# Summing two and a half of six modulation weights on GpSimd instead of VectorE

## The reference, cut to what matters

```python
mod_x = (jax.nn.silu(c) @ w_mod[i] + b_mod[i])[:, None, :]     # 1024 -> 6144
sh1x, sc1x, g1x, sh2x, sc2x, g2x = jnp.split(mod_x, 6, axis=-1)
hx = modulate(rmsnorm(x, norm1_g[i]), sh1x, sc1x)
...
x = x + g1x * out_x
hx2 = modulate(rmsnorm(x, norm2_g[i]), sh2x, sc2x)
x = x + g2x * peer(hx2, ...)
```

## Time and profile before

| | us |
|---|---|
| median of 3 runs | 1464.42 |
| profiled execution, whole | 1466.92 |
| its span | 1464.9 |
| TensorE busy | 1320.8 |
| VectorE busy | 1109.2 |
| ScalarE busy | 636.5 |
| GpSimd busy | 311.1 |

### The profile page before, as it was taken

One profiled execution on the slowest core, in us unless ns is written; L12 is line 12 of the kernel. 1 busy time (PEld: TensorE's weight loads), 2 busy tenths in 40 slices (PEclk: granted clock), 3 DMA queues, 4 the chain that ended last, 5 costly groups with the idle time before them and its releaser, 6 DMA issues.

```text
span 1464.9 us, 16512 instructions
## 1 busy us (share of the span) xinstructions
PE 1320.8 (90%) x5504; PEld 879.2 (60%) x5504; DVE 1109.2 (76%) x2316; ACT 636.5 (43%) x1322; POOL 311.1 (21%) x308
## 2 busy tenths in 40 slices
PE   9998899897897979697987799999999999999998
PEld 3876655453342534253443346678888877788887
DVE  6688857966767776776667677869997577799974
ACT  5344733322222222222222126567776445777752
POOL 0000004344444333344434330001110000011100
PEclk9999999999898989898898899999999999999999
DMA  9624468999999999999999996434445434355540
GB/s 394 268 115 195 158 246 346 415 421 422 419 421 421 422 421 421 420 412 421 418 421 400 417 386 262 172 116 171 174 174 200 160 118 157 115 182 200 193 144 29
DMA packets 50436, 416.31 MB, mean 284 GB/s; under 512 B 5552, under 2 KB 5680, under 8 KB 7088
## 3 DMA queue, kind: packets, MB, share of 16 engines
q0 software_dynamic: 36864, 268.45, 44.3%
q1 hardware_dynamic: 13488, 146.82, 26.2%
HBM read 414.20 MB, written 1.05 MB: 283 GB/s over the span
## 4 chain that ended last, share of the span: by engine, by line
PE 54%; DVE 21%; DMA 15%; issue 5%; ACT 3%; POOL 2%; DVEq 0%; SPq 0%; POOLq 0%; ACTq 0%
PE ps L1510 11%; PE ps L1223 9%; DMA ring<-in_uv,ids 8%; PE ps L1512 6%; DMA arena<-in_uv,ids 5%; PE ps L1302 4%; PE ps L1304 4%; PE ps L1303 4%; DVE ring L2260 4%; DVE arena L2260 2%; DMA ring<-in_b1w 2%; PE ps L1045 2%; PE ps L934 2%; PE ps L936 2%; PE ps L935 2%
## 5 line engine op out<-in xcount | busy, mean ns | idle before, releaser
L1223 PE MATMUL ps<-ring,arena 128*128 128x512 f32 x632 | 297.3, 621 | 53.1 <-ACT arena L1736 53.1
L2260 DVE CUSTOM_DVE_ANT_0 ring<-ring,arena 128x1024 f32<-128x1024 f32 x158 | 190.5, 1223 | 84.9 <-DMA ring<-in_uv,ids 84.2
L1223 PEld LDWEIGHTS ps<-ring,arena 128*128 128x128 f32 x632 | 123.7, 199 | 216.3 <-issue 152.4
L1510 PE MATMUL ps<-hpair,arena_r 128*128 128x512 f32 x704 | 249.0, 399 | 0.0
L617 DVE TENSOR_TENSOR arena_r<-ring,arena_r 128x1024 fp32r<-128x1024 f32 x152 | 185.6, 1224 | 61.3 <-ACT arena_r L602 58.5
L1223 PE MATMUL ps<-arena 128*128 128x512 f32 x392 | 189.2, 628 | 47.3 <-ACT arena L1736 47.1
L819 POOL DMA_INDIRECT ring<-in_uv,ids x158 | 168.5, 1066 | 233.7 <-PE ps L1223 176.3
L1512 PE MATMUL ps<-hpair,arena_r 128*128 128x256 f32 x704 | 198.0, 281 | 0.0
L602 ACT ACTIVATE arena_r<-ring 128x1024 fp32r<-128x1024 f32 x152 | 159.2, 1054 | 60.0 <-PE ps L1304 57.9
L819 POOL DMA_INDIRECT arena<-in_uv,ids x98 | 104.4, 1065 | 353.6 <-issue 240.2
L1223 PEld LDWEIGHTS ps<-arena 128*128 128x128 f32 x392 | 77.9, 202 | 150.2 <-issue 92.9
(11 more groups left out here) (337 smaller groups left out, 2037.5 us busy)
## 6 DMA issues: line engine op xcount, KB each, us to landing
ring<-in_lw SPq DMA_DIRECT2D x39, 2048.0 KB, 7.8
ring<-in_b1w SPq DMA_DIRECT2D x14, 2048.0 KB, 8.7
ring<-in_b1w SPq DMA_DIRECT2D x9, 1024.0 KB, 16.9
ring<-in_lw SPq DMA_DIRECT2D x8, 1024.0 KB, 5.1
wqb<-in_wq SPq DMA_DIRECT2D x4, 1024.0 KB, 9.0
arena<-in_wq SPq DMA_DIRECT2D x3, 1024.0 KB, 13.4
ring<-in_uv,ids POOLq DMA_INDIRECT x158, 16.8
ring<-in_lw SPq DMA_DIRECT2D x2, 1088.0 KB, 10.0
```

The lines of the kernel that those rows point to most:

```text
L1223: last = nc.tensor.matmul(ps[:, 4 + 2 * c + b, :], diag[:, k % 4, :], vrows[place(n, k)][:, b * 512:(b + 1) * 512], start=(n == c and k == 0),
L1510: nc.tensor.matmul(ps[:, bank, :].rearrange("p (t n) -> p t n", t=2), high_of(l, p)[:, cols_], hpair[:, :, k, :], start=(k == 0), stop=Fal ...
L2260: V.tensor_tensor_reduce(out=urows[at], in0=urows[at], in1=hrow[:, c, :], scale=1.0, scalar=0.0, op0=ALU.mult, op1=ALU.add, accum_out=dots ...
```

## The change

Weights 1 and 3 and the second half (k = 4 to 7) of weight 5 are summed by GpSimd in accumulator 1; weights 0, 2, 4 and the first half of weight 5 by VectorE in accumulator 0. GpSimd's sum uses two instructions for a part, a product into a new buffer `mterm` (the number of the partition is spread over 512 columns by a broadcast) and an addition to the accumulator; only the first part of a weight is one instruction. With 8 + 8 + 4 parts that is 15 + 15 + 7 = 37 `TENSOR_TENSOR` instructions of 128x512, each waiting for the one before. VectorE is left with 28 parts: 8 in the projection instead of 13, 3 behind it instead of 8, and 17 instead of 27 in the attention loop. The waits of SyncE and TensorE on a weight's sum go over to the new semaphore `mod_steps_pool` for weights 1, 3 and (beside the old one) 5. TensorE adds both accumulators for weight 5, in twice the instructions.

```diff
-MODB_EARLY = 21
-MODB_PARTS = (2, 2, 2, 2, 2, 2, 2, 2, 3, 3, 3, 2, 0, 0, 0, 0)
+MODB_EARLY = 11
+MODB_DVE = [(i, k) for i in (0, 2, 4, 5) for k in range(4 if i == 5 else 8)]
+MODB_PARTS = (2, 2, 1, 1, 1, 1, 1, 1, 1, 2, 2, 2, 0, 0, 0, 0)
...
+        mterm = sb("mterm", [P, 512])[:, :]
...
+        def mod_summed(eng, i):
+            if i not in (1, 3):
+                eng.wait_ge(mod_sum, (KD, 0, 2 * KD, 0, 3 * KD, 3 * KD + KD // 2)[i])
+            if i in (1, 3, 5):
+                eng.wait_ge(mod_steps_pool, (0, 2 * KD - 1, 0, 4 * KD - 2, 0, 5 * KD - 3)[i])
...
         def mod_part(dve, *parts):
             for p in parts:
-                i, k = p // KD, p % KD
-                acc, weight = macc[:, i % 2, :], slot(MODB_SLOT[i])[:, k, :]
+                i, k = MODB_DVE[p]
+                acc, weight = macc[:, 0, :], slot(MODB_SLOT[i])[:, k, :]
                 if k == 0:
                     wait_slot(dve, MODB_SLOT[i])
-                    dve.wait_ge(modcol_done, max(MOD_A, MOD_A + i - 1))
+                    dve.wait_ge(modcol_done, MOD_A + (0, 0, 1, 0, 3, 5)[i])
...
+        def mod_part_pool(pool, i, ks, steps):
+            acc = macc[:, 1, :]
+            wait_slot(pool, MODB_SLOT[i])
+            pool.wait_ge(modcol_done, MOD_A + i - 1)
+            for k in ks:
+                weight, scale = slot(MODB_SLOT[i])[:, k, :], sil2[:, k, 0:1].broadcast_to([P, 512])
+                if k == ks[0]:
+                    nc.gpsimd.tensor_tensor(acc, weight, scale, ALU.mult).then_inc(mod_steps_pool, 1)
+                else:
+                    nc.gpsimd.tensor_tensor(mterm, weight, scale, ALU.mult).then_inc(mod_steps_pool, 1)
+                    steps += 1
+                    pool.wait_ge(mod_steps_pool, steps)
+                    nc.gpsimd.tensor_tensor(acc, acc, mterm, ALU.add).then_inc(mod_steps_pool, 1)
+                steps += 1
+                pool.wait_ge(mod_steps_pool, steps)
+            return steps
...
+            pool.wait_ge(silu_ready, 2)
+            steps = mod_part_pool(pool, 1, range(KD), 0)
+            steps = mod_part_pool(pool, 3, range(KD), steps)
+            mod_part_pool(pool, 5, range(KD // 2, KD), steps)
             pool.wait_ge(first_ids, 1)
...
-                pe.wait_ge(mod_sum, KD * (i + 1))
+                mod_summed(pe, i)
...
                 for jj in range(4):
-                    last = nc.tensor.matmul(ps[:, bank, 2 * jj:2 * jj + 2], macc[:, i % 2, jj * P:(jj + 1) * P],
-                                            ones[:, 0:2], start=True, stop=True)
+                    for a in range(2) if i == MOD_B - 1 else (i % 2,):
+                        last = nc.tensor.matmul(ps[:, bank, 2 * jj:2 * jj + 2], macc[:, a, jj * P:(jj + 1) * P],
+                                                ones[:, 0:2], start=(a == 0 or i < MOD_B - 1),
+                                                stop=(a == 1 or i < MOD_B - 1))
```

More of the change, by code:

```diff
@@ L375, in program @@
         tile_done, tile_act, tile_dve = sem("tile_done"), sem("tile_act"), sem("tile_dve")
-        sil4_ready, mod_sum = sem("sil4_ready"), sem("mod_sum")
+        sil4_ready, mod_sum, mod_steps_pool = (sem(n) for n in ("sil4_ready", "mod_sum", "mod_steps_pool"))
         a_raw, a_hi, a_lo, a_used = sem("a_raw"), sem("a_hi"), sem("a_lo"), sem("a_used")
@@ L737, in b1_used @@
                 else:
-                    sp.wait_ge(mod_sum, KD * (MODB_SLOT.index(n) + 1))
+                    mod_summed(sp, MODB_SLOT.index(n))
             def l_used(l, j):
@@ L2048, in rotated @@
                 dve.wait_ge(proj_dve, count)
-            mod_part(dve, 0, 1, 2, 3)
+            mod_part(dve, 0, 1, 2)
             dve.wait_ge(in_used, in_end(0))
@@ L2053, in _ @@
             in_rest(dve, 7)
-            mod_part(dve, 4, 5)
+            mod_part(dve, 3)
             in_rest(dve, 8)
-            mod_part(dve, 6, 7)
+            mod_part(dve, 4)
             rotated(0, 3, 2)
             in_rest(dve, 9, 10)
-            mod_part(dve, 8, 9, 10)
+            mod_part(dve, 5, 6)
             in_rest(dve, 11)
-            mod_part(dve, 11, 12)
+            mod_part(dve, 7)
             heads_norm1(dve, V, run, variance, newton, rotate, cos1, sin1, rt, lambda p: in_rest(dve, p))
@@ L2073, in _ @@
             mod_bias(MOD_A, 4)
-            mod_part(dve, *range(13, MODB_EARLY))
+            mod_part(dve, *range(8, MODB_EARLY))
             leave(dve, ops_qk(), T_QK, 1, base=TURN_BANK)
@@ L2134, in _ @@
                     heads_variance(0)
-            assert part_at == KD * MOD_B
+            assert part_at == len(MODB_DVE)
             def square_of_chunk1():
```

## The result

| | before | after |
|---|---|---|
| median of the runs, us | 1464.15 (1462.68 to 1464.97, 4 runs) | 1482.55 (1480.9 to 1484.82, 4 runs) |
| ratio, 95% interval | | 1.0118 [1.0106, 1.0131] |
| profiled execution, span | 1464.9 | 1479.0 |
| start of the first gather in it | 223.19 | 241.11 |

What follows compares the result with a forecast made beforehand. Projection bound by TensorE, VectorE close behind; the loop by a chain of waits through both. Terms -2.0 + 0.84 + 0.2 + 3.0 + 4.3 + 1.0 = +7.3 us gave 1471.7 us from the median 1464.4, range 1463 to 1478.

Steps and rivals of the forecast that it cites:

- The relief: Attention loop: parts taken off VectorE in the chain at units 3, 5 and 10 save 0.76, 0.50 and 0.76, -2.0 us.
- The other seven lie beside TensorE's turn: Attention loop: seven of ten removed parts are hidden beside TensorE's turn and values; worth 0, up to 5.3 us if not.
- the rival that counted all ten: Attention loop: all ten removed parts count, -7.6 + 0.84, and no holding back; 1457.7 us, chance 0.06.
- GpSimd is too slow: Attention loop, unit 6: weight 3's sum takes 32 us and TensorE waits 7 us more; 1477 us, chance 0.14.
- the circle: Attention loop: the chain of waits through VectorE and TensorE and back to the next maximum, about 7.7 us for two units.
- the rival that the two hardly meet: VectorE is not the last to arrive where GpSimd holds it back; only -2.0 + 0.84 + 0.2 is left, 1463.4 us, chance 0.20.
- the projection's term: Projection: twelve of weight 1's GpSimd instructions fall among VectorE's work and hold it back; +3.0 us, between 0.7 and 4.3.
- 4.3 + 1.0: Attention loop: GpSimd holding VectorE back costs +4.3 us during weight 3 and +1.0 us during weight 5, units 7 to 10.
- Together 1.3 us a circle: Attention loop, weight 3: two waits of VectorE behind GpSimd, 0.45 and 0.85 us, over about 3.3 circles make +4.3 us.
- nearer to 6: Attention loop: the size of the 4.3 us term if, by the skill's rule, each small L2082 could be held as well.
- L702's successor at 91 instead of 88 us: Projection: sign expected in the changed profile, the instruction behind VectorE's L702 starting later, for the +3.0 us.
- No lateness even at 32 us, and the loads behind it come sooner: Projection: GpSimd's sum of weight 1 is in time for TensorE and for SyncE's loads of slots 12 and later.

Runs made afterwards that it cites:

- Run 4: The changed kernel with GpSimd's sums replaced by small fills and weight 0's parts back at their places of before; 1466.42 us, 1.0006 of before.
- Runs 3: The changed kernel with weight 0's eight parts back at their places of before, GpSimd's work kept; 1481.66 us, 1.0115 of before.
- run 5: The kernel before plus GpSimd's 37 products and additions on constants, at the changed kernel's points, nobody waiting for them; 1484.21 us, 1.0118 of before.

## Why the prediction was wrong in size

- **What bounds, and what is removed.** The relief was put at -2.0 with +0.84 and +0.2 on TensorE behind it, -1.0 in all. Run 4 is at 1.0006 [0.9994, 1.0018] of before, that is between 0.9 us less and 2.6 us more, and its trace shows some 0.3: the relief was smaller than forecast, if there was any. "The other seven lie beside TensorE's turn" held: they brought nothing, and the rival that counted all ten fell (its -7.6 should have been -7.3 by the terms above it, which changes nothing). This sets the ceiling for taking these twenty parts off VectorE: with GpSimd's work gone and no load late there was nothing to gain, so no other arrangement was tried for a version that beats before.
- **GpSimd's own speed.** Right: 1.04 and 1.27 us against 1.36, weight 3 in 20 us (144.25 to 164.3) against 22, TensorE not waiting for it. The rival "GpSimd is too slow" did not come.
- **The turns.** The mechanism is as forecast: whole instructions, in the projection and in the circle; the rival that the two hardly meet did not come. The size was the step that failed, in both terms. Runs 3 and 4 differ in GpSimd's work alone: up to the first maximum by 9.2 us, where the projection's term was +3.0, and from there to the first gather by 8.9, where 4.3 + 1.0 stood; 18.1 in all against 8.3.
- **The loop's term.** "Together 1.3 us a circle" took the chain's two-input instructions only and gave two of them a wait; in fact four were held, 3.2 us. The first was L2115, one input, 128x2, which the sum had let pass. The prediction had weighed a rule that says so, and put its result, "nearer to 6", beside the sum instead of into it. It would have been 1.7 us of the missing 11. That the holds in the chain still come near to the forecast's 5.3 (3.2 for weight 3, and 1.0 for weight 5, where L524 at 178.56 takes 1.80 instead of 0.76) is luck: the chain has them in one circle and not in 3.3, since VectorE waits for a slow TensorE in the next.
- **The clock.** The forecast has no term for it. A delay of VectorE becomes a wait of TensorE of 4.4 us, and what follows runs at half the clock: 3.0 us in the transposes, values and scores of that one circle, 5.4 us with the total and the two steps behind them. Unit 2's circle is 13.3 us from L2128 to L2128 (151.05 to 164.37) against 8.5 before. Holds and clock do not simply add up: with the waits filled VectorE meets GpSimd more often, and the loop still loses 7 to 8 us.
- **The projection.** "L702's successor at 91 instead of 88 us": it stood at 93.10, 4.85 us late instead of 3.0. Up to the first maximum of the loop it was 9.1 us, since behind L729 came the wait for piece 14, and slow stretches (0.91 in the rows above). "It is not caught up later" was right, but it grew, by 4.2 us.
- **SyncE's queue.** "No lateness even at 32 us, and the loads behind it come sooner" looked at weight 1, which GpSimd took over. For slot 12 it is right (about 91 instead of 118 us), but weight 0's parts were spread over later places, though the listing of the change shows only two parts gone: those that stay in their places are earlier parts of weight 0 than before. Slot 10's load waits for that one, and slots 11 and 12 stand behind it in the queue. In a kernel without turns this is worth 7.3 us, in this one no more than the 0.6 that can't be told from nothing.
- **The range** ended at 1478, since the highest terms were added one by one for turns alone; neither the clock nor the load was among them.

What stays open: the share of the clock within the 18.1 us. The filled waits put it at 3 to 4 us, with overlapping intervals, and they removed it in three places and not everywhere. Why the stretch behind the first gather differs by up to 8 us between profiles, and why run 5's executions lie between 1482.5 and 1489.4, no run shows.

## What to carry to other kernels

Work moved from VectorE to GpSimd is not free, even where GpSimd idles. Ask of every VectorE instruction on the chain, beside which GpSimd would stand, whether it reads two operands in SBUF or is a TENSOR_SCALAR, down to two columns, and charge each with a wait of up to a whole GpSimd instruction; then ask whether TensorE waits for it, and look whether the stretch behind it will run at the lower clock. And where a change spreads an accumulation over later places, look for the loads that wait for its last part, and for those queued behind them.

## What the runs showed of the hardware

- GpSimd's TENSOR_TENSOR of 128x512 takes 1.27 us, and 1.04 us with one operand broadcast from a single column; 128x128 takes 0.46 and 0.40 us alone, and 0.65 and 0.57 us on average beside VectorE's work.
- A GpSimd that only writes (128x1024 fills, 961 ns) leaves VectorE's two-input instructions alone (749 ns) and holds TENSOR_SCALAR (484 to 663 ns; 169 to 261 ns at 128x2). One that reads holds both, and leaves a TENSOR_TENSOR with one operand in PSUM (691 ns) and TENSOR_REDUCE (1224 ns) alone.
- A step of 0.17 us on two columns was held for 0.97 us. In the chain the smallest instruction can pay the most.
- Behind 4.39 us without work TensorE's granted clock was 0.50 from 152 to 164 us; with products of zeros in the wait it was 1.00 there.
